# Moving the storing of weight sums in block 0 of a hybrid encoder kernel by one step of ScalarE

## The chip, the cores and the metric

The kernel runs on one core of one Trainium2 chip. The metric is device time in microseconds (us), the median of several runs. Engines go by the profile's names: PE multiplies matrices, DVE is VectorE, ACT is ScalarE, POOL is GpSimd, SP is SyncE, which here only issues loads.

## The reference

One inference step of a one-layer encoder over 2048 prompt frames and 32 sample frames of width 1024, in float32:

```python
h = h + merge(pool_branch(n), attention(n))        # n = rmsnorm(h) through one input projection
h = h + square(relu(rmsnorm(h) @ w_up)) @ w_down   # w_up (1024, 4096), w_down (4096, 1024)
y = rmsnorm_final(h)
```

Caches and pooling states are returned as well; the change does not touch them.

## The kernel before

Activations lie with features on the 128 partitions and frames along the free axis. The frames are worked in four blocks of 512 (the last has the 32 sample frames too). Each block has a mixer (36 products with one 128 x 1024 weight unit each) and an MLP. In the MLP the 4096 hidden features are taken in four quarters `q`, each with 8 "up" units and 8 "down" units.

Every float32 weight is used as a sum of two parts, a rounded high part and a low part. A unit is loaded by SP into one of four places of `raw`; ACT copies it with rounding (`split_high`, L857), DVE subtracts to get the low part (`split_low`, L1307), and PE makes three products for each 128 x 128 tile (high x high, high x low, low x high; L576).

Blocks 1 to 3 form their MLP products with Strassen-like sums of weight quarters. These sums are made once, during the MLP of block 0, which itself multiplies plainly. The MLP of block 0 has 64 units, n = 0 to 63, and 32 pairs p, of units 2p and 2p+1. What is done for a pair:

- POOL (`sum_weights`, L1833 to L1846): when both units have landed, and when the stores of pair p-2 out of the same buffer `wsum[p % 2]` have landed (semaphore `set_out`), four additions or subtractions of 128 x 512.
- ACT (`sums_high`, L1034): waits for POOL's last one. In the up phases, and in the last down phase (`SPLIT_PHASES`, 20 pairs), it copies three sums rounded into `wsplit` (L857) and issues the store of the fourth (L1040). In the other three phases (12 pairs) it only issues the store of all four (L1042).
- DVE (`sums_low`, L1542), only for the 20 split pairs: waits for ACT's copy, makes the low parts (L1307, `wsplit<-wsum,wsplit`), in step 2p.
- ACT (`sums_out`, L1044), split pairs only, in step 2p+1: waits for DVE and issues the store of both parts (L1049).

The order on each engine is written out by hand. "Step n" is what ACT and DVE issue after the wait for product n (`wait_plain(n)`). In each step ACT first makes the high part of unit n+2, then the work on product n, and then calls `sums_step(n)`. DVE takes product n out of PSUM, makes the low part of unit n+2, does its further work, and ends with `sums_low(n)`. An up step's further work is two squares on ACT (L1070, L1071) and the low part of the hidden activations on DVE. In the last eight steps (56 to 63, down units of the last quarter) it is the next block's normed input (`nH` on ACT, `nL` on DVE, L1349) and the squares of the output: ACT's square of tile i (L883) goes into one PSUM bank and waits until DVE has added tile i-1 to `acc` (L1330); once all are added, PE sums `acc` over the partitions with a product with `ones`.

SP loads unit m when its place in `raw` is free: after the low part of unit m-4, and after POOL's sums of that unit's pair (`raw_place_free`, L471).

Of the kernel before, what the change touches and what calls it, by code (L numbers as in the profile page):

```python
# [73 lines left out]
PAIRS = 4  # L74
PHASES = 2 * NQ
# [37 lines left out]
def build(nc, x_blocks, x_last, weights, consts, vectors, tables, state_s, kcache_t, vcache, kold, vold,  # L113
          y_blocks, y_last, k_new, v_new, p_new, k_old_out, v_old_out, ks_new, vs_new, ps_new):
    with ExitStack() as ctx:
# [250 lines left out]
        def wait(eng, signal, *item):  # L366
            eng.wait_ge(signal.sem, signal.count[item])
# [487 lines left out]
        def _(act):  # L855
            def copy(out, in_, scale=1.0):
                return nc.scalar.activation(out, in_, ACT.Copy, scale=scale)  # L857
# [176 lines left out]
            def sums_high(p):  # L1034

                st, split = p % 2, p // PAIRS in SPLIT_PHASES
                wait(act, s_S, p)
                if split:
                    copy(wsplit[st][:, :, 0, :], wsum[st][:, 0:3, :]).then_inc(s_SH.sem, 1)
                    act.dma_start(sums_d[p, :, 3, :], wsum[st][:, 3, :]).then_inc(set_out[st], 16)  # L1040
                else:
                    act.dma_start(sums_d[p], wsum[st][:, :, :]).then_inc(set_out[st], 16)  # L1042

            def sums_out(p):  # L1044
                ph = p // PAIRS
                if ph in SPLIT_PHASES:
                    wait(act, s_SL, p)
                    at = SPLIT_PHASES.index(ph) * PAIRS + p % PAIRS
                    act.dma_start(split_d[at], f(wsplit[p % 2][:, :, :, :])).then_inc(set_out[p % 2], 16)  # L1049

            def sums_step(n):
                if n % 2:
                    sums_out(n // 2)
                    if n // 2 + 1 < PHASES * PAIRS:
                        sums_high(n // 2 + 1)

            def plain_split_ahead(n):
                if n < 2 * KD * NQ:
# [4 lines left out]
            def plain_up(q):  # L1063
                for i in range(KD):
                    m, n = ORD[i], 16 * q + i
                    wait_plain(act, n)
                    plain_split_ahead(n + 2)
                    act.wait_ge(relu_done, hid(q, i))
                    y = prod[i % 2][:, 1, :]
                    nc.scalar.activation(midH[:, m, 0:TB], y, ACT.Square).then_inc(hid_high, 1)  # L1070
                    nc.scalar.activation(y, y, ACT.Square).then_inc(hid_sq, 1)  # L1071
                    sums_step(n)

            def plain_down(q):
                for i in range(KD):
                    n = 16 * q + KD + i
                    wait_plain(act, n)
                    plain_split_ahead(n + 2)
                    if q == 0:
                        if i == 0:  # L1080
                            act.wait_ge(x_in, 16)
                        square("x", 1, i, xT)
                    if q == NQ - 1:
                        gained_high("x", 1, i)
                        if i == 0:
                            root("x", 1)
                        act.wait_ge(down_added, hid(q, i))
                        square("f", 0, i, hT)
                    sums_step(n)
# [916 lines left out]
```

## Time and profile before

| what | value |
|---|---|
| median of 3 runs | 2337.78 us (2336.32 to 2338.15) |
| the profiled execution's own time | 2337.89 us |
| its span, first to last instruction | 2336.1 us |
| PE busy | 2313.3 us, 99% of the span |
| DVE, ACT, POOL busy | 1622.5, 1080.1, 358.3 us |
| granted TensorE clock, mean | 0.999 |

The profile is of one execution; its span leaves out what lies around the first and the last instruction. A row of the timeline gives an instruction's start (us from the start of the span), its duration, and in brackets how long its engine was idle before it and what ended that. Matmuls overlap, so their durations add to more than the time they take; the distance of their starts is what counts.

### The profile page before, as it was taken

Reading aid. Unit: us, or ns where it says so; the run is one execution under the profiler, and the core shown is the slowest. Engines: PE = TensorE matmul, PEld = TensorE weight load, DVE = VectorE, ACT = ScalarE, POOL = GpSimd, SP = SyncE. Lnnn points to the kernel's source line nnn. Section 1 sums busy time; section 2 is a strip of 40 time slices with the busy share of each in tenths; the row PEclk is TensorE's granted clock in tenths of the full one; section 3 lists DMA queues with packets and bytes.
Section 4 is the critical chain, followed back from the end, with each engine's and each line's share of the span. In section 5 each row is a group of like instructions: output and inputs, shape, how many; then the busy total and the mean of one; then the engine's idle time right before and its main releaser. Section 6 shows DMA issues by size and latency. Waiting matters only on the chain.

```text
span 2336.1 us, 38106 instructions
## 1 busy us (share of the span) xinstructions
PE 2313.3 (99%) x14855; PEld 2078.5 (89%) x14855; DVE 1622.5 (69%) x2472; ACT 1080.1 (46%) x1915; POOL 358.3 (15%) x280
## 2 busy tenths in 40 slices
PE   8999999999999999999999999999999999999998
PEld 6788788888777899999977889999999999999998
DVE  7655755557865677866885568778687556867867
ACT  4533433425343365654534346546543434644544
POOL 0400457566241000000004000000002300000001
PEclk9999999999999999999999999999999999999999
DMA  4223657556522366677731237766753122676674
GB/s 164 81 83 103 224 213 264 198 211 239 216 82 79 102 240 215 208 231 230 239 130 63 97 108 263 245 210 212 246 192 112 63 93 94 230 236 197 205 235 170
DMA packets 150498, 410.18 MB, mean 176 GB/s; under 512 B 17328, under 2 KB 19728, under 8 KB 146224
## 3 DMA queue, kind: packets, MB, share of 16 engines
q1 hardware_dynamic: 113088, 261.30, 33.9%
q10 hardware_dynamic: 37232, 146.45, 17.9%
q8 instruction: 119, 1.95, 0.3%
q14 instruction: 59, 0.48, 0.1%
HBM read 349.65 MB, written 58.13 MB: 175 GB/s over the span
## 4 chain that ended last, share of the span: by engine, by line
PE 97%; DMA 1%; DVE 1%; POOL 0%; issue 0%; ACT 0%; SPq 0%; DVEq 0%; POOLq 0%; ACTq 0%
PE prod L576 51%; PE auxB L811 8%; PE auxB L813 8%; PE auxB L812 8%; PE prod L811 6%; PE prod L813 6%; PE prod L812 6%; PE auxB L576 1%; PE auxA L689 1%; PE auxB L719 1%; PE auxB L703 1%; PE auxA L576 0%; DMA wring<-weight_split 0%; DMA raw<-weights 0%; DVE acc L1330 0%; DMA weight_split<-wsplit 0%
## 5 line engine op out<-in xcount | busy, mean ns | idle before, releaser
L576 PE MATMUL prod<-nH,wm 128*128 128x512 f32 (+1 forms) x2592 | 710.8, 363 | 9.9 <-DVE nL L1349 7.9
L857 ACT ACTIVATE wm<-raw 128x1024 fp32r<-128x1024 f32 x232 | 235.5, 1015 | 657.5 <-PE prod L576 649.4
L576 PEld LDWEIGHTS prod<-nH,wm 128*128 128x128 f32 x2592 | 449.4, 188 | 94.9 <-DVE wm L1307 10.6
L576 PE MATMUL prod<-nL,wm 128*128 128x512 f32 (+1 forms) x1296 | 433.7, 361 | 0.0
L857 ACT ACTIVATE wring<-rawq 128x512 fp32r<-128x512 f32 x492 | 303.4, 629 | 259.3 <-PE auxB L813 164.4
L1307 DVE TENSOR_TENSOR wring<-rawq,wring 128x512 fp32r<-128x512 f32 x492 | 335.0, 685 | 96.1 <-PE auxB L813 79.5
L1307 DVE TENSOR_TENSOR wm<-raw,wm 128x1024 fp32r<-128x1024 f32 x232 | 302.8, 1305 | 69.4 <-ACT wm L857 68.9
L576 PE MATMUL prod<-midH,wm 128*128 128x512 f32 (+1 forms) x1152 | 324.2, 370 | 0.3 <-DVE wm L1307 0.3
L576 PEld LDWEIGHTS prod<-nL,wm 128*128 128x128 f32 x1296 | 230.8, 188 | 38.5 <-issue 1.0
L576 PEld LDWEIGHTS prod<-midH,wm 128*128 128x128 f32 x1152 | 204.2, 188 | 39.8 <-issue 0.9
L576 PE MATMUL prod<-midL,wm 128*128 128x512 f32 (+1 forms) x576 | 202.5, 370 | 0.0
L1865 POOL COPY xb<-carry 128x16 f32<-128x16 f32 x12 | 2.3, 194 | 1034.5 <-DVE xb L1424 538.8
L811 PE MATMUL auxB<-n7H,wring 128*128 128x256 f32 x512 | 145.5, 284 | 0.0
L811 PE MATMUL auxB<-m7H,wring 128*128 128x256 f32 x512 | 145.2, 284 | 0.3
L813 PE MATMUL auxB<-n7H,wring 128*128 128x256 f32 x512 | 144.9, 283 | 0.0
L812 PE MATMUL auxB<-n7L,wring 128*128 128x256 f32 x512 | 144.9, 283 | 0.0
L812 PE MATMUL auxB<-m7L,wring 128*128 128x256 f32 x512 | 144.9, 283 | 0.0
L813 PE MATMUL auxB<-m7H,wring 128*128 128x256 f32 x512 | 144.9, 283 | 0.0
L576 PEld LDWEIGHTS prod<-midL,wm 128*128 128x128 f32 x576 | 104.2, 188 | 19.8 <-issue 0.2
L1758 DVE TENSOR_TENSOR hT<-hT,auxB 128x256 f32<-128x256 f32 (+1 forms) x184 | 77.6, 422 | 48.5 <-PE auxB L813 47.4
L811 PE MATMUL prod<-m7H,wring 128*128 128x256 f32 x384 | 109.7, 286 | 0.1
L811 PE MATMUL prod<-n7H,wring 128*128 128x256 f32 x384 | 109.5, 285 | 0.0
(239 smaller groups left out, 5167.0 us busy)
## 6 DMA issues: line engine op xcount, KB each, us to landing
raw<-weights SPq DMA_DIRECT2D x200, 512.0 KB, 3.3
wring<-weight_split ACTq DMA_DIRECT2D x171, 512.0 KB, 4.7
rawq<-weights SPq DMA_DIRECT2D x288, 256.0 KB, 3.6
rawq<-weight_sums SPq DMA_DIRECT2D x204, 256.0 KB, 4.0
weight_split<-wsplit ACTq DMA_DIRECT2D x20, 1536.0 KB, 5.5
weight_sums<-wsum ACTq DMA_DIRECT2D x12, 1024.0 KB, 5.2
raw<-weights SPq DMA_DIRECT2D x32, 320.0 KB, 2.9
y_blocks<-hT ACTq DMA_DIRECT2D x12, 512.0 KB, 2.7
```

Source lines behind the costliest of these rows:

```text
L576: ins = nc.tensor.matmul(out[:, s, 0:hi - lo], lhs, rhs[:, lo:hi], start=first, stop=last)
L689: ins = nc.tensor.matmul(bank[:, at:at + P], q, keys[:, :, t * CH:(t + 1) * CH], start=True, stop=True)
L703: ins = nc.tensor.transpose(auxB[:, 1, i * P:(i + 1) * P], pr[:, c % 2, i * P:(i + 1) * P], ident)
L719: ins = nc.tensor.matmul(auxB[feats, 0, 0:2 * P], v[:, c // 2, feats], prT[:, c % 2, 2 * g * P:2 * (g + 1) * P], start=True, stop=True)
L811: nc.tensor.matmul(out, wh, xh, start=kp == 0 and (r in (1, 2, 5) or (final and r == 4)), stop=False, skip_group_check=True)
L812: nc.tensor.matmul(out, wh, xl, start=False, stop=False, skip_group_check=True)
L813: ins = nc.tensor.matmul(out, wl, xh, start=False, stop=kp == PAIRS - 1, skip_group_check=True)
L857: return nc.scalar.activation(out, in_, ACT.Copy, scale=scale)
L1307: return tt(out, x, f(high), ALU.subtract)
L1758: tt(h, h, bank_c(b, j) if r == 5 else bank_a(b, j), ALU.add).then_inc(s_add.sem, 1)
L1865: link(nc.gpsimd.tensor_copy(x[:, 0:16], carry[:, g, :]) if b > 0 else nc.gpsimd.memset(x[:, 0:16], 0.0))
```

## The change

`sums_high` of a pair was called at the end of step 2p-1, behind `sums_out` of the pair before; for pair 0 it is called ahead of step 0, and stays there. It is now called at the end of step 2p, behind that step's `split_high` and its work on the product. `sums_out` and `sums_low` keep their steps.

```diff
             def sums_step(n):
                 if n % 2:
                     sums_out(n // 2)
-                    if n // 2 + 1 < PHASES * PAIRS:
-                        sums_high(n // 2 + 1)
+                elif n > 0:
+                    sums_high(n // 2)
```

## Rows read from the trace of the kernel before

**Rows 1.** The page: busy us of each engine, share of the span, instructions.
```profile
PE 2313.3 (99%) x14855; PEld 2078.5 (89%) x14855; DVE 1622.5 (69%) x2472; ACT 1080.1 (46%) x1915; POOL 358.3 (15%) x280
```

**Rows 2.** Windows of 40 us in block 0's MLP: busy us, granted clock, DMA.
```profile
272.00:312.00 40.00, 40.00 (x174) 32.44 (x173) 25.17 (x24) 15.69 (x20) 29.85 (x18) 1.00 0.76 282
...
592.00:632.00 40.00, 36.68 (x154) 28.26 (x153) 31.72 (x37) 14.79 (x20) 6.93 (x4) 1.00 0.65 234
```

**Rows 3.** Waits between 240 and 620 us: total, times, longest.
```profile
POOL wsum L1843 <- DMA weight_split<-wsplit: 117.3, 18, 19.4
...
ACT wsplit L857 <- POOL wsum L1846: 18.5, 9, 3.0
```

**Rows 4.** PE's timeline around the end of block 0.
```profile
593.00 0.47 PE L576 MATMUL prod<-midH,wm 128*128 128x512 f32 x1 [0.27 <-DVE wm L1307]
...
603.90 0.40 PE L576 MATMUL prod<-midH,wm 128*128 128x512 f32 x1
605.90 0.50 PE L576 MATMUL prod<-nH,wm 128*128 128x512 f32 x1 [1.61 <-DVE wm L1307]
...
611.23 0.50 PE L576 MATMUL prod<-nH,wm 128*128 128x512 f32 x1 [0.18 <-DVE nL L1349]
...
613.45 1.10 PE L576 MATMUL auxA<-acc,ones 128*128 128x512 f32 x2 [1.25 <-DVE acc L1330]
```

**Rows 5.** ACT's timeline, steps 59 to 62.
```profile
589.17 1.48 ACT L857 ACTIVATE wsplit<-wsum 128x1536 fp32r<-128x1536 f32 x1
590.55 1.04 ACT L857 ACTIVATE wm<-raw 128x1024 fp32r<-128x1024 f32 x1
...
594.20 0.60 ACT L883 ACTIVATE auxA<-hT 128x512 f32<-128x512 f32 x1 [2.00 <-DVE acc L1330]
...
602.16 1.49 ACT L857 ACTIVATE wsplit<-wsum 128x1536 fp32r<-128x1536 f32 x1 [1.15 <-POOL wsum L1846]
...
603.55 1.04 ACT L857 ACTIVATE wm<-raw 128x1024 fp32r<-128x1024 f32 x1
```

**Rows 6.** DVE's timeline, steps 58 to 62.
```profile
579.98 1.75 DVE L1307 TENSOR_TENSOR wsplit<-wsum,wsplit 128x1536 fp32r<-128x1536 f32 x1
...
594.03 1.75 DVE L1307 TENSOR_TENSOR wsplit<-wsum,wsplit 128x1536 fp32r<-128x1536 f32 x1
...
596.29 1.72 DVE L1307 TENSOR_TENSOR wm<-raw,wm 128x1024 fp32r<-128x1024 f32 x1
597.93 1.78 DVE L1349 SCALAR_TENSOR_TENSOR nL<-xT,vec,nH 128x512 fp32r<-128x512 f32 x1
...
604.62 1.23 DVE L1307 TENSOR_TENSOR wm<-raw,wm 128x1024 fp32r<-128x1024 f32 x1 [3.71 <-ACT wm L857]
605.77 0.74 DVE L1349 SCALAR_TENSOR_TENSOR nL<-xT,vec,nH 128x512 fp32r<-128x512 f32 x1
```

**Rows 7.** POOL's timeline, pair 31 (the first two of its four instructions).
```profile
595.03 1.90 POOL L1843 TENSOR_TENSOR wsum<-raw 128x512 f32<-128x512 f32 x1 [5.94 <-DMA weight_split<-wsplit]
597.01 2.15 POOL L1844 TENSOR_TENSOR wsum<-wsum,raw 128x512 f32<-128x512 f32 x1
```

**Rows 8.** DVE's timeline, steps 38 and 39 (end of an up phase).
```profile
468.95 2.24 DVE L1307 TENSOR_TENSOR wsplit<-wsum,wsplit 128x1536 fp32r<-128x1536 f32 x1
...
473.35 0.68 DVE L1307 TENSOR_TENSOR midL<-prod,midH 128x512 fp32r<-128x512 f32 x1
```

**Rows 9.** PE's timeline: the first matmul of unit 40.
```profile
469.67 0.39 PE L576 MATMUL prod<-midH,wm 128*128 128x512 f32 x1
```

**Rows 10.** The instructions on `wsum`: times to landing of its stores.
```profile
DMA to landing us min/median/max: 2.4/5.3/9.7
```

**Rows 11.** ACT's timeline, steps 11 and 12 (a phase without split).
```profile
314.34 0.33 ACTq L1042 DMA_DIRECT2D weight_sums<-wsum  x1
...
319.86 1.06 ACT L857 ACTIVATE wm<-raw 128x1024 fp32r<-128x1024 f32 x1 [3.98 <-PE prod L576]
```

**Rows 12.** POOL's timeline, start of pair 8.
```profile
320.65 1.30 POOL L1843 TENSOR_TENSOR wsum<-raw 128x512 f32<-128x512 f32 x1 [1.32 <-DMA raw<-weights]
```

## The prediction, made before the changed kernel was run

> **What bounds the kernel now.** First the page: PE is busy 99% of the span [rows 1], so an edit on ACT gains only where PE stands still. Then the windows of block 0's MLP: in the middle PE works 40.00 of 40 us, from 592 to 632 us only 36.68 [rows 2]; the clock granted is 1.00 in both. So all that this change can give back lies in the last stretch. PE's timeline there shows where. Units 62 and 63 begin to end run from 593.00 to 603.90, 47 starts apart, 0.232 us each, so a unit of 24 matmuls is 5.57 us [rows 4]. Unit 62 starts 0.4 us late (idle 0.27 plus the overlap that is lost). The product after unit 63 could start at 604.13 and starts at 605.90: 1.8 us, waiting for DVE's low part. Its last tile waits for `nL` (0.35 us late), and the sum with `ones` for `acc` (1.4 us late) [rows 4]. Together 4.0 us: the most that could be gained, if all four stalls went.
>
> The waits view says why the change is tempting: ACT stands 18.5 us, nine times, for POOL's last sum [rows 3]. One of these is the 1.8 us: ACT waits for POOL until 602.16, copies pair 31 for 1.49 us, and only then makes the high part that PE stands still for, at 603.55 [rows 5], so DVE's low part comes at 604.62 [rows 6]. The other eight cost PE nothing, since it has no idle time there [rows 2].
>
> **The change, part by part.** No instruction or DMA is added or removed; 19 copies of 1.48 us and 31 issues of stores (of the 20 and 32; pair 0 stays) move one step later on ACT's queue.
>
> *Taken away:* behind `sums_out` in odd steps, the copy and its wait for POOL. High parts of even units come earlier; in step 62 that of unit 64 by what is left after the rest has moved (below).
>
> *Added:* a wait on DVE. Before, the low part of a pair followed straight behind DVE's own work, as the copy was a step old: at 579.98 and 594.03, 1.75 us each [rows 6]. Now ACT copies behind its square, and in the last eight steps that square waits for DVE's addition to `acc`, which is just what DVE does ahead of the low part. So DVE adds, ACT squares (0.60), ACT copies (1.48) [rows 5], and only then DVE may go on: 2.2 us of standing, with the handovers, in steps 58, 60 and 62. Behind the waiting instruction stand the next step's `hT` addition, the low part of the next unit, for which PE waits, and `nL` and `acc`, for which ACT's next square waits.
>
> Whether it costs more depends on POOL. When POOL adds at the same time, `split_low` took 1.72 us and `nL` 1.78, against 1.23 and 0.74 when it does not; POOL's own additions took 1.90 and 2.15 instead of 1.30 [rows 6, 7, 12]. In `nL`'s case the order is seen: it starts at 597.93 inside POOL's 597.01 to 599.16 and ends 0.55 behind that. POOL will still be at pair 31 when unit 63 is split, since it starts on the landing of a store that does not come earlier. So I take the long durations; the short ones are the other bound.
>
> The Trainium skill (SBUF — State Buffer, section "Who interferes with whom") says that a VectorE instruction with two SBUF inputs and a GpSimd instruction that reads SBUF don't share: the second one waits out the first. By that rule the sum below is its upper variant, by the undisturbed durations its lower one; the trace's 1.78 against 0.74 us agrees with the rule.
>
> The sum, step by step, from the rows' starts:
> - Step 58: DVE's low part of pair 29 starts at about 581.9 instead of 579.98; with POOL's pair 30 in the way it ends some 2.4 us later than before. ACT is 1.4 us freer in step 59, as no copy of pair 30 stands there (589.17 to 590.65 before), but its square waits for DVE's chain, which is now 1.4 us late (1 us of standing in step 59 is used up). So the high part of unit 62 starts at 590.55 as before: a gain on ACT spent on DVE. Unit 62 starts at 593.0 again.
> - Step 60: ACT's square 594.20 to 594.80, then the copy of pair 30 to 596.20. DVE's low part starts at 596.23 instead of 594.03, ends at 597.9, or 598.8 if POOL's first addition (about 596) is ahead of it.
> - Step 61: `hT` 0.68, then the low part of unit 63: done at 599.7 undisturbed, 600.3 to 601.2 with POOL. PE wants it at 593.00 + 5.57 = 598.57. New stall: 1.1, or 1.8 to 2.6 us.
> - Then `nL`, `acc`, ACT's square, and without a copy in between the high part of unit 64 at 601.7, or 603.3 to 604.2 (603.55 before), low part done at 604.0, or 605.9 to 606.5; unit 63 ends at 605.3, or 605.9 to 606.8. So the 1.8 us stall is gone: PE starts that product at about the old 605.90, within 0.9 us.
> - Step 62: `nL`, `acc`, square, copy of pair 31, low part of pair 31, step 63's `hT`, low part of unit 65, `nL`, `acc`, square, `acc`: the same chain as before plus 2.2 us of standing, less what DVE stood in step 62 before (3.71 us for ACT [rows 6], now about 1). PE's `ones` product then starts at 613.9 undisturbed, at 615.6 to 616.2 with POOL, against 613.45 [rows 4].
>
> The sum: +0.5 us as lower variant, +2.1 to +2.8 as upper. I take +2.3, as the additions of unit 63's step are those that ran against POOL in the rows. 2336.1 + 1.8 around it is the profiled 2337.89; +2.3 gives 2340.2. The profiled execution lies 0.1 above the median 2337.78, so the forecast is 2340.1.
>
> *Costed at nothing, with the cover:*
> - The up phases. ACT copies behind its second square instead of a step ahead, so DVE's low part comes up to 0.7 us later, then the next step's work. The tightest place is the start of a down phase: unit 40 starts at 469.67, its last tile is due 21 matmuls later, at 474.5, and the low part of the hidden tile it needs ends at 474.03 [rows 8, 9]: 0.5 us of cover. There DVE starts pair 19's low part at 468.95, and the copy would end by 468.7, so nothing moves. Without that cover it is up to 0.7 us at each of four such places.
> - The phases without split. A store of all four sums goes 5.5 us later, for pair 6 from 314.34 to behind 319.86 and ACT's high part, about 320.9 [rows 11]. It lands 5.3 us later [rows 10], at 326.2, and POOL starts pair 8 then instead of at 320.65 [rows 12]. POOL's end goes to about 332.5. Late next would be SP's load of units 20 and 21; their places are only free after steps 14 and 15 (from 330.9), and unit 20 is needed in step 18, at 353. Cover: some 17 us.
>
> **The rivals.**
> - *The gain stays.* DVE's standing is covered by slack, the low part of unit 63 comes by 598.6, and the 1.8 us goes, with up to 1.7 more behind it. For it: DVE stood 3.71 us for ACT in step 62 [rows 6]; against it: the chain of square, copy and low part has no slack in step 60. Time: 2337.8 less 1.8 to 3.5, 2334.3 to 2336.0.
> - *POOL's round gets too long* (the slow side). Two stores of a pair must land before POOL starts the pair after next; POOL stood 117.3 us for the second [rows 3], so this is a closed round of two pairs, four steps, 22.3 us: POOL 6 to 8, ACT's copy at its new place up to 3.6 into a step, DVE to the step's end, store and landing some 7.5. It closes with about 3 us left. It decides from the point at which POOL's sums come more than 2 us into the pair's own even step: ACT then stands in front of the next high part. A round 1 us too long on each of the ten returns of the 20 split pairs would cost 10 us: 2348. Against it: POOL's wait now lands a step ahead of where it is needed.
> - *Nothing moves.* The tail is set by DVE's and ACT's chain whatever order they have: within 0.5 us, 2337.8 to 2338.3. This is the lower variant above.
>
> **How the numbers follow.** The forecast with both variants, +0.3 to +2.9 us, has 0.75; the gain that stays 0.12; POOL's round 0.05; the rest lies between or is a stall in the up phases of 1 to 3 us (0.08). The time is 2340.1. The range reaches down to 2336.6, half into the gain, for the runs before spread by 1.8 us, and up to 2342.2, where one or two of the up phases' stalls are added: what is left out is some 0.1 below and 0.07 above. A change counts here from 0.2%, 4.7 us, about what can be told from no change. Faster by that would need more than all 4.0 us of PE's standing in this stretch: 0.01. Slower by that needs POOL's round: 0.05. Within it: 0.94.
>
> **What would show it.** Right: ACT no longer waits for POOL's sum; DVE waits some 2 us for ACT's `wsplit` copy in steps 58, 60 and 62; PE's stall ahead of the product after unit 63 is gone and one of 1 to 2.6 us stands ahead of unit 63; 40.00 of 40 us in the middle. Wrong: no stall ahead of unit 63 (then the gain stays), or PE idle before 590 us (then a round or an up phase fails).

## The result, and the profile after

The changed kernel takes 2341.84 us (median of 20 runs, 2340.66 to 2343.45) against 2337.82 us before (20 runs, 2336.32 to 2338.86): ratio 1.0017, 95% interval 1.0011 to 1.0023. It is 4.0 us slower, inside the stated range of 2336.6 to 2342.2 and inside the 0.2% that were called no change; of the 4.0 us the forecast had 2.3.

The page of the changed kernel, its span and its busy times:
```profile
span 2339.3 us, 38106 instructions
...
PE 2314.2 (99%) x14855; PEld 2079.1 (89%) x14855; DVE 1621.3 (69%) x2472; ACT 1079.8 (46%) x1915; POOL 360.7 (15%) x280
```
The work is the same (POOL is busy 2.4 us longer, every other engine within 1.2 us of before); the span is 3.2 us longer in this execution. The windows say where (busy us of PE, PEld, DVE, ACT, POOL, then the granted clock):
```profile
272.00:312.00 40.00, 40.00 (x174) 32.41 (x173) 25.87 (x24) 15.61 (x20) 30.94 (x19) 1.00 0.76 279
592.00:632.00 40.00, 34.19 (x138) 25.89 (x137) 28.52 (x32) 16.03 (x21) 6.87 (x4) 0.96 0.60 224
```
The middle is as full as before [rows 2], and nothing has moved by its end: the matmul that starts at 587.72 us before starts at 587.75. At the end of block 0 PE is busy 34.19 us instead of 36.68, and the clock is no longer full: 0.96. Those are two separate losses.

The waits between 240 and 625 us (total, times, longest):
```profile
POOL wsum L1843 <- DMA weight_split<-wsplit: 104.6, 18, 19.8
...
POOL wsum L1843 <- DMA weight_sums<-wsum: 37.2, 12, 5.5
...
DVE wsplit L1307 <- ACT wsplit L857: 10.8, 11, 2.1
```
ACT's 18.5 us of waiting for POOL [rows 3] are gone. Two waits are new: DVE's for ACT's copy, and POOL's for the stores that now leave a step later. Only the first of them costs anything (experiment 1). DVE's timeline, steps 58 to 62, shows how:
```profile
581.88 1.92 DVE L1307 TENSOR_TENSOR wsplit<-wsum,wsplit 128x1536 fp32r<-128x1536 f32 x1 [2.14 <-ACT wsplit L857]
...
584.32 1.72 DVE L1307 TENSOR_TENSOR wm<-raw,wm 128x1024 fp32r<-128x1024 f32 x1
...
596.90 1.76 DVE L1307 TENSOR_TENSOR wsplit<-wsum,wsplit 128x1536 fp32r<-128x1536 f32 x1 [2.13 <-ACT wsplit L857]
...
599.17 1.71 DVE L1307 TENSOR_TENSOR wm<-raw,wm 128x1024 fp32r<-128x1024 f32 x1
600.81 1.77 DVE L1349 SCALAR_TENSOR_TENSOR nL<-xT,vec,nH 128x512 fp32r<-128x512 f32 x1
...
604.89 1.23 DVE L1307 TENSOR_TENSOR wm<-raw,wm 128x1024 fp32r<-128x1024 f32 x1 [1.11 <-ACT wm L857]
...
609.51 1.76 DVE L1307 TENSOR_TENSOR wsplit<-wsum,wsplit 128x1536 fp32r<-128x1536 f32 x1 [2.14 <-ACT wsplit L857]
```
Three times DVE stands 2.1 us, where it went straight on before [rows 6]; the third of those, in step 62 of the kernel before, was
```profile
607.03 1.75 DVE L1307 TENSOR_TENSOR wsplit<-wsum,wsplit 128x1536 fp32r<-128x1536 f32 x1
```
The wait of 3.71 us in step 62 has become 1.11. And unit 63's low part (599.17) and the `nL` behind it run against POOL again, at the long durations. ACT's timeline shows the same chain from the other side:
```profile
591.20 1.04 ACT L857 ACTIVATE wm<-raw 128x1024 fp32r<-128x1024 f32 x1
...
594.86 0.60 ACT L883 ACTIVATE auxA<-hT 128x512 f32<-128x512 f32 x1 [2.00 <-DVE acc L1330]
...
595.39 1.47 ACT L857 ACTIVATE wsplit<-wsum 128x1536 fp32r<-128x1536 f32 x1
...
603.81 1.05 ACT L857 ACTIVATE wm<-raw 128x1024 fp32r<-128x1024 f32 x1
```
The copy for pair 30 stands behind a square that itself stood for DVE. PE's timeline, to be held against [rows 4]:
```profile
593.65 0.47 PE L576 MATMUL prod<-midH,wm 128*128 128x512 f32 x1 [0.90 <-DVE wm L1307]
...
601.03 0.47 PE L576 MATMUL prod<-midH,wm 128*128 128x512 f32 x1 [1.60 <-DVE wm L1307]
...
606.63 0.39 PE L576 MATMUL prod<-nH,wm 128*128 128x512 f32 x1
...
613.72 0.50 PE L576 MATMUL prod<-nH,wm 128*128 128x512 f32 x1 [2.06 <-DVE nL L1349]
...
615.94 2.05 PE L576 MATMUL auxA<-acc,ones 128*128 128x512 f32 x2 [1.25 <-DVE acc L1330]
617.00 1.42 PE L576 MATMUL prod<-nH,wm 128*128 128x512 f32 x1
```
The stall of 1.61 us ahead of the product after unit 63 is gone (606.63), one of 1.60 us stands ahead of unit 63 (601.03), and the wait for the last `nL` has grown from 0.18 to 2.06. The product with `ones` starts at 615.94 instead of 613.45: +2.5 us, which is what the forecast's sum says.

The second loss begins there. That product takes 2.05 us instead of 1.10 [rows 4]. The windows from 614 us on, two us each, have the granted clock in the third column from the end:
```profile
614.00:616.00 2.00, 0.75 (x4) 0.30 (x3) 1.06 (x3) 1.64 (x3) 0.00 (x0) 0.85 0.99 336
616.00:618.00 2.00, 2.00 (x3) 0.97 (x4) 1.23 (x1) 0.42 (x1) 0.00 (x0) 0.50 1.02 430
618.00:620.00 2.00, 2.00 (x8) 1.60 (x8) 1.26 (x1) 0.69 (x1) 0.00 (x0) 0.80 1.02 340
```
0.50 is the lower of the two levels, 1.2 GHz instead of 2.4. PE had stood 2.06 us and worked for about 1; the share lost in the first row puts the fall at 615.4, within the wait of 1.25 us (614.69 to 615.94). The lost shares (0.15, 0.50 and 0.20 of two us each, over 0.5) make 3.4 us at half clock. One and the same matmul behind the product with `ones`, in the kernel before and in the changed one:
```profile
616.24 0.63 PE L576 MATMUL prod<-nH,wm 128*128 128x512 f32 x2
...
620.10 0.63 PE L576 MATMUL prod<-nH,wm 128*128 128x512 f32 x2
```
It comes 3.9 us later: 1.4 us more than at 615.94. The matmuls keep this distance until 0.6 us of it is made up in the last block, around 2300 us, which the change does not touch; so the spans differ by 3.2.

### The profile page after: what moved, and what is told of

It is laid out like the page before. It is cut to its first block, busy times and chain, and to the rows that moved or that the text cites. A ratio compares the mean times of both kernels' runs of the same rounds, so it can differ in the third digit from the quotient of the medians.

```text
span 2339.3 us, 38106 instructions
## 1 busy us (share of the span) xinstructions
PE 2314.2 (99%) x14855; PEld 2079.1 (89%) x14855; DVE 1621.3 (69%) x2472; ACT 1079.8 (46%) x1915; POOL 360.7 (15%) x280
## 4 chain that ended last, share of the span: by engine, by line
PE 96%; DVE 2%; DMA 1%; ACT 1%; issue 0%; SPq 0%; DVEq 0%; ACTq 0%
PE prod L576 50%; PE auxB L811 8%; PE auxB L813 8%; PE auxB L812 8%; PE prod L811 6%; PE prod L813 6%; PE prod L812 6%; PE auxB L576 1%; PE auxA L689 1%; PE auxB L719 1%; PE auxB L703 1%; PE auxA L576 0%; DVE acc L1330 0%; DVE wm L1307 0%; DMA wring<-weight_split 0%; DVE nL L1349 0%
```

## The experiments

Two theories stood against each other. A: the whole loss arises in steps 58 to 64, from DVE's wait for a copy that stands behind ACT's square, and from the clock that falls behind PE's waits there. B: the 27 pairs moved in the middle, with their later stores, have a part in it. Differences are to the median of the kernel before on the same chip; the 95% interval of an experiment's median reaches about 2 us to either side. Edits are shown against the changed kernel where nothing else is said.

**1. The change for pairs 1 to 27 alone.**
```diff
                 if n % 2:
                     sums_out(n // 2)
-                elif n > 0:
+                    if 55 <= n < 63:
+                        sums_high(n // 2 + 1)
+                elif 0 < n < 56:
                     sums_high(n // 2)
```


> The change for pairs 1 to 27 alone; pairs 28 to 31, of the last eight steps, in the order of before. Theory A (all of the loss is made in steps 58 to 64, by VectorE's wait for the copy behind the square, and by what PE's standing there does to its clock): same as before within 0.5 us, 2337.3 to 2338.3, PE idle as before (0.3 us ahead of unit 62, 1.6 ahead of the product after unit 63, 0.2 and 1.25 behind). Rival B (the 27 moved pairs in the middle, with their later stores, cost something too, by transfers or by POOL's round): 1 us or more above before.

2337.34 us against 2338.12, ratio 0.9997 (0.9989 to 1.0006). PE's waits are those of before:
```profile
605.28 0.50 PE L576 MATMUL prod<-nH,wm 128*128 128x512 f32 x1 [1.62 <-DVE wm L1309]
...
610.60 0.50 PE L576 MATMUL prod<-nH,wm 128*128 128x512 f32 x1 [0.19 <-DVE nL L1351]
...
612.82 1.10 PE L576 MATMUL auxA<-acc,ones 128*128 128x512 f32 x2 [1.25 <-DVE acc L1332]
```
The idle times agree with [rows 4] to 0.01 us. The median's interval alone (2.6 us below to 1.4 above) would leave room for a cost of 1 us; PE's timeline does not: even the changed kernel, with all of these pairs moved, gains or loses less than 0.2 us against before between 230 and 588 us. B falls: later copies and stores cost nothing that shows in the middle.

**2. The change for pairs 29 to 31 alone.**
```diff
                 if n % 2:
                     sums_out(n // 2)
-                elif n > 0:
+                    if n <= 55:
+                        sums_high(n // 2 + 1)
+                elif n > 56:
                     sums_high(n // 2)
```


> The change for pairs 29 to 31 alone. Theory A: the whole loss, +3.5 to +4.5 us against before, with the stalls of the changed kernel (0.9, 1.6, 2.1 and 1.25 us) and a stretch of half clock behind them. Rival B: less than +3 us, the rest of the loss being in the pairs left as before.

2341.53 us, +3.4, ratio 1.0014 (1.0006 to 1.0023), just under the expected +3.5 to +4.5; the interval reaches down into B's range, but PE's idle times are those of the changed kernel, 0.75, 1.60, 2.03 and 1.25 us. With experiment 1: these three copies carry the loss. The clock is low for longer than in the changed kernel's profile:
```profile
613.15 0.50 PE L576 MATMUL prod<-nH,wm 128*128 128x512 f32 x1 [2.03 <-DVE nL L1351]
...
615.37 2.04 PE L576 MATMUL auxA<-acc,ones 128*128 128x512 f32 x2 [1.25 <-DVE acc L1332]
```
```profile
614.00:616.00 2.00, 0.75 (x2) 0.50 (x2) 1.33 (x3) 1.85 (x3) 0.00 (x0) 0.56 1.05 434
616.00:618.00 2.00, 2.00 (x4) 1.00 (x3) 0.69 (x1) 0.55 (x1) 0.00 (x0) 0.50 0.96 399
618.00:620.00 2.00, 2.00 (x6) 1.54 (x5) 1.83 (x1) 0.14 (x1) 0.00 (x0) 0.50 0.88 287
620.00:622.00 2.00, 2.00 (x8) 1.54 (x8) 1.52 (x1) 0.00 (x0) 0.00 (x0) 0.73 0.30 123
```
The same lost shares make 6.8 us here, against 3.4. They also date the fall: the first row lost 0.44 of two us, so half clock began at 614.24, when the wait for `acc` (614.12 to 615.37) was 0.1 us old. Here it was not the second wait that lowered it.

So the clock's part differs between executions with the same stalls, and the runs of the changed kernel on record bear that out. Eight of the 20 list a mean granted clock of 0.998, as its profiled execution does; their median is 2341.2 us. Twelve list 0.997, as the execution profiled here does; their median is 2342.4. Of the 66 runs of the kernel before that were taken beside these experiments, none lists less than 0.998.

**3. ACT's copy ahead of its square, in the last eight steps.** The square stands some 2 us for DVE anyhow; the copy goes into that time. ACT's `plain_down` of the changed kernel becomes:
```diff
+                        if n % 2 == 0:
+                            sums_step(n)
                         act.wait_ge(down_added, hid(q, i))
                         square("f", 0, i, hT)
-                    sums_step(n)
+                    if n % 2 or q < NQ - 1:
+                        sums_step(n)
```


> The changed kernel, but in the even ones of the last eight steps ScalarE copies ahead of its square, in the 2 us in which the square waits for VectorE's addition. Theory A: VectorE no longer waits for the copy, the high parts of units 62 and 64 come 1 to 3 us earlier, and PE stands only ahead of the product with ones (about 1.5 us); 2 to 3 us below before, 2335 to 2336, full clock throughout. Rival C (the copies' place does not matter; POOL's additions against VectorE's set the end of block 0): within 1 us of the changed kernel, +3 to +4.5 against before.

2336.38 us, 1.7 below before, ratio 0.9993 (0.9984 to 1.0002), and 5 to 6 us below the changed kernel. C falls: the place of the copy decides. But the expectation missed in its time (2335 to 2336) and in two points of the profile, which is of a run of 2338.1 us, where seven of the eleven took 2336.45 or less. DVE still waits once, in step 62:
```profile
592.97 1.75 DVE L1310 TENSOR_TENSOR wsplit<-wsum,wsplit 128x1536 fp32r<-128x1536 f32 x1
...
605.15 1.76 DVE L1310 TENSOR_TENSOR wsplit<-wsum,wsplit 128x1536 fp32r<-128x1536 f32 x1 [2.12 <-ACT wsplit L857]
```
Pair 30's low part goes straight on (592.97); pair 31's waits, since ACT's copy now reaches the point before POOL is done, and holds the square behind it. ACT's timeline:
```profile
603.62 1.49 ACT L857 ACTIVATE wsplit<-wsum 128x1536 fp32r<-128x1536 f32 x1 [3.62 <-POOL wsum L1849]
```
And PE stands twice, with the lower clock behind it (the product with `ones` takes 1.83 us):
```profile
609.36 0.50 PE L576 MATMUL prod<-nH,wm 128*128 128x512 f32 x1 [1.25 <-DVE nL L1352]
...
611.60 1.83 PE L576 MATMUL auxA<-acc,ones 128*128 128x512 f32 x2 [1.28 <-DVE acc L1333]
```

**4. Filling matmuls in the changed kernel.** PE makes 14 products that nobody reads, into a bank that is free then.
```diff
+                    if (b, i, k) == (1, 0, 7):
+                        fill(i, 9)
                     if i == 0:
                         wait(pe, s_nL, "x", b, k)
...
+                    if (b, i, k) == (1, 1, 0):
+                        fill(i, 5)
                     if b > 0 and (i, k) == (1, 0):
                         sum_squares("f", b - 1)
...
+            def fill(i, n):
+                for _ in range(n):
+                    nc.tensor.matmul(auxB[:, 0, :], wm[0][:, i % 2, 0, 0:P], nH[:, 0, 0:TB], start=True, stop=True)
```


> The changed kernel with 14 matmuls on PE whose result nobody reads: 9 (2.1 us) ahead of its wait for the last nL, 5 (1.2 us) ahead of its wait for the last acc. Theory A (part of the loss is the half clock behind two waits in a row): the clock stays at full through 615 to 620 us, the product with ones takes 1.1 instead of 2.05 us, and the time is 1.2 to 1.6 us below the changed kernel, +2.4 to +2.8 against before. Rival D (the slow matmuls there have another cause, or the waits themselves cost all): the changed kernel's time, +3.5 to +4.5.

2339.25 us, +1.1, ratio 1.0007 (0.9998 to 1.0016): 2.9 us less than the changed kernel's +4.0, with 14 matmuls more. The windows that had 0.50 and 0.80 of the clock:
```profile
616.00:618.00 2.00, 2.00 (x8) 1.30 (x8) 1.53 (x2) 1.18 (x3) 0.00 (x0) 1.00 1.00 424
618.00:620.00 2.00, 2.00 (x10) 1.61 (x9) 2.00 (x1) 0.00 (x0) 0.00 (x0) 1.00 0.87 344
```
The stall ahead of unit 63 is still there (1.62 us) and the product with `ones` starts at 615.80, as in the changed kernel (615.94); but the matmul that stood at 620.10 there now starts at 618.62, 2.4 us later than before. So the first loss stays and the second is gone. The median's +1.1 lies below this profile and below the expected +2.4 to +2.8, by less than its interval of 2 us. So 2.9 us is a rough figure for the clock's part: by the starts of the matmuls behind `ones`, the profiles give 1.4 us in the changed kernel and 2.7 in experiment 2.

**5. Fill ahead of `nL` alone.** Experiment 4 without the second `fill`.

> The changed kernel with the 9 filling matmuls ahead of the wait for the last nL alone; the wait of 1.25 us for acc stays, as in the kernel before. Theory A: that wait alone did not lower the clock before and does not now: full clock, +2.3 to +2.9 us against before. If the wait for acc alone lowers it here: +3.5 to +4.5.

2339.46 us, +1.7, ratio 1.0006 (0.9997 to 1.0015), below the expected +2.3 to +2.9 by less than the interval, and full clock behind the 1.25 us for `acc`:
```profile
615.61 1.10 PE L576 MATMUL auxA<-acc,ones 128*128 128x512 f32 x2 [1.25 <-DVE acc L1336]
```
In this profile a wait of that length alone lowers nothing, as in the kernel before, and nine of the eleven runs list a mean clock of 0.999.

**6. Fill ahead of `acc` alone.** Experiment 4 without the first `fill`.

> The changed kernel with the 5 filling matmuls ahead of the wait for acc alone; PE's wait of 2.06 us for the last nL stays. If it takes two waits in a row to lower the clock: full clock, +2.3 to +2.9 us against before. If the longer wait alone does: half clock for some us, +3.5 to +4.5.

2340.69 us, +2.9, ratio 1.0010 (1.0001 to 1.0019), between the two expected ranges. In the profile the clock stays full behind the wait of 2.04 us:
```profile
613.54 0.51 PE L576 MATMUL prod<-nH,wm 128*128 128x512 f32 x1 [2.04 <-DVE nL L1355]
```
```profile
614.00:616.00 2.00, 2.00 (x9) 1.31 (x8) 1.02 (x4) 1.82 (x3) 0.00 (x0) 1.00 0.95 354
```
But this profile is of a run of 2339.8 us. Five of the eleven took 2339.4 to 2340.1, six took 2340.7 to 2341.3, about 1.2 us more, which is close to the 1.4 us of half clock above; in experiment 5, where the product with `ones` starts at the same time (615.61 and 615.56), ten of eleven stayed at or below 2339.92. Only three of the eleven list a clock of 0.999, against nine there. So the wait of 2.04 us alone probably lowers the clock in some executions, as the fall in experiment 2's profile suggests too. No trace shows it here, and that it takes two waits in a row is not shown.

**7. The change for pair 31 alone.**
```diff
                 if n % 2:
                     sums_out(n // 2)
-                elif n > 0:
+                    if n < 61:
+                        sums_high(n // 2 + 1)
+                elif n == 62:
                     sums_high(n // 2)
```


> The change for pair 31 alone. Theory A: PE's stall of 1.6 us ahead of the product after unit 63 goes, but VectorE's chain ends at most 0.3 us earlier, so that the wait moves to the last nL (about 1.2 us) and to acc (about 1.5 us); two waits in a row, so perhaps half clock behind them. Time -0.5 to +1.5 us against before. Rival (the gain stays: the stall that the change takes away was worth its 1.8 us): 1.5 to 2 us below before.

2338.55 us, +0.8, ratio 1.0003 (0.9995 to 1.0012). This is the part of the change that takes the 1.6 us stall away, and nothing is left of it: PE has no idle time ahead of the product after unit 63, which starts 1.7 us earlier than before, and then
```profile
610.94 0.50 PE L576 MATMUL prod<-nH,wm 128*128 128x512 f32 x1 [1.69 <-DVE nL L1351]
...
613.15 1.10 PE L576 MATMUL auxA<-acc,ones 128*128 128x512 f32 x2 [1.25 <-DVE acc L1332]
```
it stands 1.69 us for `nL` instead of 0.18. The product with `ones` starts 0.3 us earlier than before [rows 4], as expected. The clock held here behind two waits, in a run of 2337.0 us. The runs spread from 2336.35 to 2341.78, wider than those of any other kernel, and two of them (2339.83 and 2341.78) list a mean clock of 0.997, which no run of the kernel before does: in some executions it fell here too. So the median says little about the 0.3 us; the timeline shows them.

**8. Experiment 3 with pair 31 wholly behind.** ACT copies pair 31 behind the last square, DVE makes its low part behind the last addition to `acc`, the store follows in step 63. Against experiment 3, in `sums_step` and `sums_low`:
```diff
+                if n == 63:
+                    sums_high(31)
                 if n % 2:
                     sums_out(n // 2)
-                elif n > 0:
+                elif 0 < n < 62:
                     sums_high(n // 2)
...
-                if n % 2 == 0 and p // PAIRS in SPLIT_PHASES:
+                if (n == 63 or n % 2 == 0 and n < 62) and p // PAIRS in SPLIT_PHASES:
```


> As the kernel with ScalarE's copy ahead of its square, and pair 31 wholly behind: ScalarE copies it behind the last square of step 63, VectorE makes its low part behind the last addition to acc, the store follows there. Theory A (the end of block 0 is VectorE's chain, and every low part of sums in it is paid in PE's waits): PE's waits at the end of block 0 fall from 4.0 us to under 0.7, full clock, 3 to 4 us below before, 2334 to 2335. Rival C (POOL's additions against VectorE's set the end): not below the kernel with the copy ahead of the square, 1 to 2 us below before.

2334.72 us against 2337.75, 3.0 below before, ratio 0.9985 (0.9976 to 0.9994), and faster than both kernels. Of PE's waits at the end of block 0 one is left, and the clock is full:
```profile
610.52 1.10 PE L576 MATMUL auxA<-acc,ones 128*128 128x512 f32 x2 [1.17 <-DVE acc L1335]
```
That wait is longer than the 0.7 us expected. DVE now makes pair 31's low part behind it, where nothing waits for it:
```profile
610.94 1.76 DVE L1312 TENSOR_TENSOR wsplit<-wsum,wsplit 128x1536 fp32r<-128x1536 f32 x1 [0.71 <-ACT wsplit L857]
```

## Why the prediction was right, and what it left out

*Where the time could change.* Right. Only the last stretch of block 0 moved; 40.00 of 40 us in the middle, and experiment 1 puts the change in the middle at no measurable cost. POOL does stand for the later stores (37.2 us in total; pair 8 starts at 324.40, forecast 326.2), and the cover that was named holds: no load came late enough for PE to see.

*DVE's new wait.* Right: 2.2 us forecast, 2.14, 2.13 and 2.14 measured, in steps 58, 60 and 62.

*Steps 58 and 59.* Off by 0.65 us. DVE's chain was to be 1.4 us late at the square of step 59; it was 2.0 late (the square starts at 590.66, before at 588.63), so the high part of unit 62 came at 591.20 and not at 590.55 as before, and unit 62 started 0.65 us later than before. The forecast let DVE win back 1 us of standing in step 59. Only about 0.5 was there, and the low part of unit 61 (584.32) ran against POOL for 1.72 us, where it had taken 1.23 before.

*Steps 60 and 61.* Right in sum, by two errors that offset each other: unit 63's low part was due at 600.3 to 601.2 with POOL and was done at 600.9; PE started the unit at 601.03. The low part of pair 30 started 0.67 us after the forecast 596.23, from the step before; but POOL's first addition, expected at about 596, came at 597.98, so this low part took 1.76 us and not the 0.9 more of the upper end. That part is luck. The choice of the long durations was right: 1.71 and 1.77 us, against 1.22 and 0.75 in step 63, where POOL is done. The Trainium skill (SBUF — State Buffer, "Who interferes with whom") has the second of the two instructions wait out the first; the trace agrees again, with `nL` at 1.77 us where it starts (600.81) inside POOL's 599.88 to 602.03.

*The stall that goes.* Right: the product after unit 63 starts without idle time, at 606.63, within the 0.9 us of the old 605.90 that the forecast gave. Experiment 7 shows why that is worth next to nothing: what is freed there is spent a few us on, at `nL` and `acc`, since DVE's chain ends within 0.3 us of when it did.

*The end of the sum.* Right: the product with `ones` was forecast at 615.6 to 616.2 and starts at 615.94. The term "+2.3" measures +2.5.

*What was left out.* The sum has no term for the clock. It counted each wait of PE at its own length and took the granted clock to stay at 1.00 as in [rows 2]. Around the waits of 2.06 and 1.25 us it fell to half, for 3.4 us in the changed kernel's profile and 6.8 in that of experiment 2: 1.4 and 2.7 us by the matmuls' starts. Experiment 4 keeps the stalls of DVE's chain, fills the other two, and the fall is gone. The chain's +2.5 and the clock's 1.4 make the 3.9 us by which the changed kernel's matmuls are late at 620 us, against the forecast +2.3 and a median of +4.0. That the time still lies in the stated range is in part luck: the forecast's own two variants ended at +2.9, and the room above them was left for stalls in the up phases, which did not come. The Trainium skill (TensorE: Matmul & The Clock Gate, "Part 1: The HAM clock gate") has the clock set by how busy PE has been; the fall to 0.50 around PE's standing, and the 1.00 with the fill, agree with it.

*The rivals.* "The gain stays" fell by the place of the copy, not by its idea: with the copy ahead of the square and the last pair out of the chain (experiment 8) the gain is there, 3.0 us; with the first alone (experiment 3) the median is 1.7 us below before, and its interval reaches 0. "POOL's round" fell with experiment 1. "Nothing moves" holds for the end of DVE's chain with pair 31 alone (0.3 us), not for the whole change.

Left open: what exactly decides whether the clock falls, how often, and for how long. Waits of 1.69 and 1.25 us in a row left it at full in one profile, waits of 1.25 and 1.28 lowered it in another; in experiment 2 it fell behind the wait of 2.03 us, in experiment 6 a wait of 2.04 left it at full in the profile.

## What to carry to other kernels

When a piece of work is moved behind another on one engine, look at what that other piece waits for: here the copy went behind a square that waits for VectorE, and so made VectorE wait for itself. A stall removed in the middle of a chain is worth only what the chain's end moves; follow it to the last consumer before counting it. And where an engine has slack time in front of a wait, that is the place for the extra work, not behind the wait, as long as the work's own input is there by then: for pair 31 it was not, and the copy held the square (experiment 3).

## What the runs showed of the hardware that was not expected

Around waits of PE of 2.06 and 1.25 us, with about 1 us of matmuls between, the granted clock fell from 2.4 to 1.2 GHz for 3.4 us, so 3.3 us of standing cost 1.4 us more. With the same waits in another kernel (2.03 and 1.25 us, experiment 2) it fell as soon as 0.1 us into the second, for 6.8 us. With both waits filled by 14 matmuls that nobody reads, the profile shows full clock, and the median was +1.1 us against before instead of +4.0, each within some 2 us (experiment 4). With one of the two filled, the profiles show full clock as well (experiments 5 and 6), but with the wait of 2.04 us left in, six of eleven runs took about 1.2 us more than the others, so that the clock probably fell in those.
